# Attention heads: turned at the end of an even period, squared and summed in the odd one, normalised tokens turned in the next even period

## What is computed

```python
h = rms_norm(x, norm_mix_g[l])
proj = h @ w_in[l]
mix_a = neighbourhood_attention(q, k, v, rpb[l])     # softmax over an 8 x 16 window of a 16 x 64 grid
mix_b = spatial_gating(z_b, ...)
mix_c = fourier_mix(x_c)
mix = head_rms_norm(concatenate([mix_a, mix_b, mix_c]), head_norm_g[l])
x = x + mix @ w_out[l]
x = x + (silu(rms_norm(x) @ w_gate[l]) * (rms_norm(x) @ w_up[l])) @ w_down[l]

def head_rms_norm(y, g):       # per token and head
    yf = yf * rsqrt(mean(yf * yf) + EPS)
```

## Time and profile before

| | |
|---|---|
| median of 3 runs | 2007.36 us (2007.29 to 2007.72) |
| the profiled execution, its own time | 2007.3 us |
| its span | 2005.5 us |
| granted TensorE clock | 0.999 |
| busy: TensorE matmul, weight load | 99%, 82% |
| busy: VectorE, ScalarE, GpSimd | 76%, 45%, 11% |
| periods 4 to 15, first layer | 223.9 to 274.9 us of the span |

### The profile page before, as it was taken

One profiled execution on the slowest core, in us unless ns is written; L12 is line 12 of the kernel. 1 busy time (PEld: TensorE's weight loads), 2 busy tenths in 40 slices (PEclk: granted clock), 3 DMA queues, 4 the chain that ended last, 5 costly groups with the idle time before them and its releaser, 6 DMA issues.

```text
span 2005.5 us, 28816 instructions
## 1 busy us (share of the span) xinstructions
PE 1981.8 (99%) x10528; PEld 1647.2 (82%) x10528; DVE 1530.2 (76%) x2511; ACT 895.3 (45%) x1611; POOL 221.0 (11%) x156
## 2 busy tenths in 40 slices
PE   8999999999999999999999999999999999999998
PEld 7887788888888888888898877888888888888887
DVE  8847874799777777787777488567997777778877
ACT  7453873443333333444544549535333333344443
POOL 1221453100000000000013123630000000000000
PEclk9999999999999999999999999999999999999999
DMA  7965743124432338533477668331343233293333
GB/s 247 214 168 154 228 156 119 43 99 170 132 110 90 106 109 288 174 98 96 120 220 193 156 159 245 138 105 58 129 157 118 90 106 110 100 342 99 95 100 122
DMA packets 130988, 288.91 MB, mean 144 GB/s; under 512 B 12960, under 2 KB 17952, under 8 KB 130592
## 3 DMA queue, kind: packets, MB, share of 16 engines
q1 hardware_dynamic: 107584, 241.97, 37.0%
q0 software_dynamic: 10880, 20.97, 6.3%
q10 hardware_dynamic: 12384, 24.12, 3.4%
HBM read 227.77 MB, written 59.24 MB: 143 GB/s over the span
## 4 chain that ended last, share of the span: by engine, by line
PE 89%; DVE 6%; issue 2%; ACT 2%; DMA 0%; DVEq 0%; SPq 0%; ACTq 0%
PE bank L2249 27%; PE bank L2251 27%; PE bank L2250 27%; PE bank L2470 1%; PE bank L2398 1%; PE bank L2547 1%; DVE s_lo L1484 1%; DVE t_lo L1913 0%; PE bank L2492 0%; PE bank L2361 0%; PE bank L2485 0%; ACT logits L1189 0%; PE bank L2377 0%; DVE logits L1772 0%; DVE att_sq L1829 0%
## 5 line engine op out<-in xcount | busy, mean ns | idle before, releaser
L2249 PE MATMUL bank<-t_hi,s_hi 128*128 128x512 f32 (+1 forms) x1336 | 516.9, 387 | 0.8 <-DVE hid_cu L2026 0.5
L2250 PE MATMUL bank<-t_lo,s_hi 128*128 128x512 f32 (+1 forms) x1336 | 516.3, 386 | 0.0
L2251 PE MATMUL bank<-t_hi,s_lo 128*128 128x512 f32 (+1 forms) x1336 | 516.3, 386 | 0.0
L2249 PEld LDWEIGHTS bank<-t_hi,s_hi 128*128 128x128 f32 x1336 | 250.9, 188 | 52.4 <-DVE hid_cu L2026 1.3
L2251 PEld LDWEIGHTS bank<-t_hi,s_lo 128*128 128x128 f32 x1336 | 250.9, 188 | 50.9
L2250 PEld LDWEIGHTS bank<-t_lo,s_hi 128*128 128x128 f32 x1336 | 251.0, 188 | 50.7
L2249 PE MATMUL bank<-b_hi,s_hi 128*128 128x512 f32 x528 | 206.0, 390 | 0.1
L2251 PE MATMUL bank<-b_hi,s_lo 128*128 128x512 f32 x528 | 205.5, 389 | 0.0
L2250 PE MATMUL bank<-b_lo,s_hi 128*128 128x512 f32 x528 | 205.4, 389 | 0.0
L992 ACT ACTIVATE s_hi<-w_u 128x512 fp32r<-128x512 f32 x142 | 89.6, 631 | 233.1 <-PE bank L2251 175.6
L992 ACT ACTIVATE s_hi<-w_down 128x512 fp32r<-128x512 f32 x154 | 97.3, 632 | 201.9 <-PE bank L2251 199.9
(11 more groups left out here) (296 smaller groups left out, 3704.8 us busy)
## 6 DMA issues: line engine op xcount, KB each, us to landing
w_raw<-in_win SPq DMA_DIRECT2D x51, 512.0 KB, 5.8
w_g<-in_wg SPq DMA_DIRECT2D x44, 512.0 KB, 3.6
w_u<-in_wu SPq DMA_DIRECT2D x44, 512.0 KB, 4.5
t_raw<-hidden_t SPq DMA_DIRECT2D x88, 256.0 KB, 2.6
w_raw<-in_win POOLq DMA_DIRECT2D x40, 512.0 KB, 7.1
t_raw<-hidden_b SPq DMA_DIRECT2D x66, 256.0 KB, 2.6
hidden_b<-hid_g SPq DMA_DIRECT2D x60, 256.0 KB, 2.0
hidden_t<-hid_x SPq DMA_DIRECT2D x44, 256.0 KB, 2.0
```

The costliest lines, as they stand in the source:

```text
L2249: nc.tensor.matmul(bank, lh, rh, start=start, stop=False, skip_group_check=reopened)
L2250: nc.tensor.matmul(bank, lh, rl, start=False, stop=False, skip_group_check=reopened)
L2251: return nc.tensor.matmul(bank, ll, rh, start=False, stop=stop, skip_group_check=reopened)
```

## The change

On all four engines the steps of the head normalisation move by part of a period. TensorE turns the heads behind `values` of the even period, and the tokens in the next even period before `values` (so both kinds of transposes stand in even periods, none in odd ones). ScalarE squares at the start of the odd period and copies the tokens behind the first exponential of the even one. VectorE sums in the odd period between `turned_even` and the second logits, and normalises at the start of the next even period. GpSimd squares the sums of the exponentials of the next tile right behind the power. In the tail, tile 5's tokens are turned there too, and `turn_heads(6)` and `turn_tokens(6)` move back. Nothing is added or taken away.

```diff
@@ GpSimd
-                for t in range(8):
+                def sums_squared(t):
                     pool.wait_ge(p_made, l * 64 + 8 * t + 8)
...
+                sums_squared(0)
+                for t in range(8):
...
                     nc.gpsimd.tensor_tensor(SR[:, 0:HA], SS[:, 0:HA], NHALF[:, 0:HA], ALU.pow).then_inc(o_rstd, 1)
+                    if t < 7:
+                        sums_squared(t + 1)
                     for n in {1: (0,), 5: (1,), 6: (2, 3)}.get(t, ()):
                         piece_lo(l, OUT_P + n)
@@ ScalarE
                 for m in range(SINGLE // 2, 16):
+                    if m % 2:
+                        head_square((m - 5) // 2)
+                    if m == 8:
+                        piece_hi(l, OUT_P)
+                    turned_odd(4 * m - 1)
+                    probs(4 * m)
                     if m % 2 == 0 and m >= 6:
                         tile_raw((m - 6) // 2)
-                    if m == 7:
-                        piece_hi(l, OUT_P)
-                    if m % 2:
-                        turned_odd(4 * m - 1)
-                        probs(4 * m)
-                    else:
-                        probs(4 * m)
-                        turned_odd(4 * m - 1)
                     probs(4 * m + 1)
-                    if m % 2 == 0 and m >= 4:
-                        head_square((m - 4) // 2)
...
-                tile_raw(5)
                 piece_hi(l, OUT_P + 1)
                 turned_odd(63)
+                tile_raw(5)
+                piece_hi(l, OUT_P + 2)
                 head_square(6)
-                piece_hi(l, OUT_P + 2)
@@ VectorE
                     if m % 2:
                         heads_copy((m - 3) // 2)
+                    elif m >= 6:
+                        head_norms((m - 6) // 2)
                     logits(4 * m)
                     if m % 2:
                         turned_even(4 * m - 2)
+                        head_sums((m - 5) // 2)
                         logits(4 * m + 1)
-                        head_norms((m - 5) // 2)
...
-                    if m % 2 == 0:
-                        head_sums((m - 4) // 2)
                     turned_even(4 * m)
+                head_norms(5)
                 turned_even(62)
+                heads_copy(7)
                 head_sums(6)
                 head_norms(6)
-                heads_copy(7)
@@ TensorE
                     turn_halves(2 * m - 1)
+                    if m % 2 == 0 and m >= 6:
+                        turn_tokens((m - 6) // 2)
+                    values(2 * m - 2)
+                    values(2 * m - 1)
                     if m % 2 == 0:
                         turn_heads((m - 4) // 2)
-                    values(2 * m - 2)
-                    values(2 * m - 1)
-                    if m % 2:
-                        turn_tokens((m - 5) // 2)
                     turn_halves(2 * m)
                 pe.wait_ge(bt_lo, l * 8 + 8)
                 out_early(0, 0, 1)
                 turn_halves(31)
-                turn_heads(6)
+                turn_tokens(5)
                 out_early(0, 4, 5)
                 values(30)
                 values(31)
+                turn_heads(6)
                 out_early(0, 2, 3)
                 out_early(1, 0, 1)
                 turn_heads(7)
+                out_early(1, 4, 5, 2, 3)
                 turn_tokens(6)
-                out_early(1, 4, 5, 2, 3)
                 out_early(2, 0, 1, 4, 5)
                 turn_tokens(7)
                 out_early(2, 2, 3)
```

## The result

The changed kernel takes 2019.2 us, the median of five runs (2019.11 to 2019.61), against 2007.36 us before, which is the median of five runs too and not of three. The ratio is 1.0059, with a 95% interval from 1.0045 to 1.0072: slower, by a little, and clear of the noise. Its profiled execution took 2019.11 us at a granted clock of 0.998, that of the kernel before 2007.3 us; the sum of the prediction, made from one profiled execution, has to explain 11.8 us and gave 11.3.

The account below looks back on a forecast made before the run. TensorE, 99% busy, was taken as the bound, with order in a ring of three nearly full engines deciding. Loop +3.2 and tail +2.4 made 5.6 us a layer, 11.3 for two: 2007.3 to 2018.6 us, range 2011.0 to 2022.0.

Parts of the forecast that it names:

- Odd period: Odd loop periods: the halves' second six transposes wait for an exponential delayed by VectorE's sums; 4.43 us, 0.05 shorter, six times.
- Even period: Even loop periods: TensorE gets the tokens' 0.58 us unhidden, plus 0.12 us of ScalarE's lateness; +0.70 us, five times.
- ScalarE's lateness: Into even periods: late exponentials delay `turned_odd`, so the halves start 1.36 us after the scores instead of 1.24; 0.12 us more.
- Tail: After the loop: GpSimd's power of tile 6 starts 2.6 us later, tile 7's tokens wait 2.0 us; +2.4 us a layer.
- only the waits go: Rival on the loop: six token waits go with nothing in their place; 2003.6 us, related VectorE-load mechanism 2002.7; chance 0.08.
- The rule of the Trainium skill: Whole kernel: judges TensorE by its weight loads, so VectorE is the engine to relieve; its gain of waits would give 2002.7 us.
- The hidden tail: Rival on the tail: loop as forecast, tail hidden but for 0.43 us; +7.3 us, 2014.6 us; chance 0.17.
- the cheap loop: Rival on the loop: odd wait half as long, paying for the even period; 2007 to 2012 us; chance 0.13.

Follow-up runs that it names:

- sums made twice: The changed kernel with VectorE's sums of squares made twice in odd periods, the first time into a spare tile: 2026.56 us, ratio 1.0094.
- the scaling ahead of the logits: The kernel before, with VectorE's scaling of the heads put ahead of the second logits in odd periods: 2009.3 us, ratio 1.001.
- The tail alone: The kernel before with only the changed kernel's tail order, tile 5's tokens staying in the loop: 2011.78 us, ratio 1.0024.
- the multiplication: The changed kernel with GpSimd's power replaced by a multiplication, so heads are not scaled as the reference's: 2015.22 us, ratio 1.0039.
- the later sums: The changed kernel with VectorE's sums behind the second logits instead of ahead of them in odd periods: 2019.83 us, ratio 1.0061.
- changed, copy on ScalarE: The changed kernel with the heads' copy moved from VectorE to ScalarE, both logits ahead of `turned_even` and the sums behind it: 2015.79 us, ratio 1.0043.
- both reliefs: The changed kernel with the heads' copy on ScalarE, logits ahead of `turned_even`, sums behind it, and a multiplication replacing GpSimd's power: 2009.49 us, ratio 1.001.

## Why the prediction was right, point by point

**Odd period: right in kind and size.** The forecast was −0.05, six times. Measured −0.23, −0.19, −0.08, −0.06, −0.13 and −0.11, together −0.80 instead of −0.3 us. The chain came as worked out link by link (period 9: 4.40 against a forecast of 4.43), and sums made twice show that it is VectorE's queue that sets it. Of the 0.5 us between them 0.32 lies in periods 5 and 7. The kernel before explains 0.15 of that: the sum took period 9, 4.48 us, for all six, and these two took 4.53 and 4.58. The rest, mostly in periods of narrower keys, which the sum left out, has no cause that a run shows.

**Even period: right, 0.07 short.** Forecast +0.70, five times; measured +0.77, +0.74, +0.74, +0.78, +0.83, together +3.86 against 3.5. The 0.58 of the tokens is bare TensorE work. ScalarE's lateness was put at 0.12. In period 8 the halves start 1.41 us after the scores, 0.17 more than before, and the scaling ahead of the logits gave 0.19.

**Period 4: a term left out.** It takes 4.43 us against 4.12. The heads were moved behind the values here too, which I left out since the period has neither tokens nor squares. TensorE in period 4 of the changed kernel:

```profile
225.46 0.88 PE L2472 MATMUL bank<-probs_t,v_band 96*64 96x128 f32 x12
226.60 0.88 PE L2472 MATMUL bank<-probs_t,v_band 96*64 96x128 f32 x12 [0.26 <-DVE probs_t L1810]
```

The second half of the values comes too early for VectorE's `turned_even`, which the heads had covered: the instruction that went had hidden a wait. The loop is thus −0.80 + 3.86 + 0.31 = +3.37 us against +3.2: three misses of 0.3 to 0.5 us that nearly cancel, so that the loop came out so close is in part luck.

**Tail: right.** Forecast +2.4, measured +2.45 (17.16 us from the first output product to the last tokens, 14.71 before). With the shift of 3.44 us taken off, the power of tile 6 starts at 282.87 (forecast 282.75). The forecast's wait of 2.0 counts from start to start; measured so it is 1.96, of which TensorE is idle for 1.80, and the extra group of transposes costs 0.49 (forecast 0.43). The tail alone (+4.4) and the multiplication (−4.0) both give 2 us a layer, so this is shown from both sides.

**Sum.** One layer is 3.37 + 2.45 = 5.82 us, two are 11.6 of the 11.8 measured. Two figures beside the sum don't follow from its terms. The lower end of the range, 2011.0, is given as the loop without ScalarE's lateness and a short tail wait, but 2 x (2.6 + 0.43) gives 2013.4. And for odd periods of 3.59 us the exponential has to be ready 3.34 us after the odd scores (3.59 − 0.20 − 0.05), not 3.1; the 3.58 us that it took before speak against that rival even so.

**The rivals.** That only the waits go is refuted: they did go, all twelve of a layer, and 11.8 us came. VectorE's busy time in the stretch fell by 1.6 us (45.3 to 43.7), 0.7 of it because tile 5's scaling now comes behind the stretch, while the time rose. The rule of the Trainium skill that I had set against the forecast (Perfetto Trace Analysis, Identifying the Most-Contended Engine) picks VectorE over the weight loads here; its gain did not come. In the kernel before, the copy taken off VectorE gave nothing outside of period 7, but it went to ScalarE, so load and order are not told apart there. They are in the changed kernel: 0.6 us more of VectorE's work in one place of the odd period cost its full length, while the same engine stood idle for 1.43 us in the even one. The hidden tail is refuted by the tail alone, and the cheap loop by the changed kernel's own periods.

**What the forecast didn't see** is how many rings lie close together. Undo the wait in the odd period by the later sums, and the time goes to 2019.83; take the copy off VectorE, and half of the gain goes into the even period, since GpSimd's power and ScalarE's exponentials are next. The traces show this best when the pairs of periods (5 and 6 up to 13 and 14) are cut elsewhere: from the odd scores to the halves behind the even scores, and from those halves to the next odd scores. Sums of the five pairs, in us:

| kernel | odd scores to even halves | even halves to odd scores |
|---|---|---|
| before | 27.90 | 14.69 |
| before, scaling ahead of the second logits | 28.71 | 14.68 |
| changed | 28.17 | 17.59 |
| changed, sums twice | 31.12 | 17.59 |
| changed, sums later | 27.51 | 18.80 |
| changed, copy on ScalarE | 25.97 | 18.81 |
| the same without the power | 25.98 | 17.57 |

The second part grew by 2.90 us, which is five times the 0.58 of the tokens. It grows once more, by 1.2, where the scaling comes late, and that goes with the power. The first part ends with ScalarE's `turned_odd`. The later sums took 2.98 us off the five odd periods, but only 0.66 off this part: the even scores come sooner, but the halves behind the even scores start nearly when they did. With both reliefs the second part is long by the tokens alone; what holds the first part is, by the trace, VectorE's sums and third logits and then ScalarE, which no run tested by itself.

## What to carry to other kernels

When three engines pass work in a ring and TensorE is nearly full, a wait in the waits' table is no prize to be had: ask which instruction of the next ring is due a moment later, and whether the move puts work in front of it. Work out the chain of starts through all engines for each of the two alternating periods apart, and follow it on into the period behind, where a shortened one can give its gain back. Count a moved instruction at full length where its queue has no gap and the ring waits for what stands behind it. For a moved piece, follow who waits for it and what is queued behind that waiter, a queue on GpSimd included; and look in the edge periods for waits that the moved work had been hiding.

## What the runs showed of the hardware

On GpSimd a power of 128 x 8 elements takes 1.64 us and a multiplication of the same tile 0.20 us: eight times as long, with no more data. That is of no matter in the changed kernel's loop and 2 us a layer in its tail. And GpSimd works its queue in order here: in the changed tail the sums of tile 7 are ready at about 289.3, but two `piece_lo` (4.76 us together) stand between the two powers, and the second one starts at 293.07.
